# Fused two-block transformer on one core: steps beside the first input product laid out by time

## The reference

```
z = rms_norm(x, norm_mix) @ w_in
y_a = rg_lru_mixer(...)        # conv of 4, two sigmoid gates, a linear scan, times gelu(gate)
y_b = short_conv_mixer(...)    # conv of 3
y_c = fox_mixer(...)           # 4 heads, causal attention with a forget gate
y_d = nsa_mixer(...)           # 4 heads: compressed, selected and window attention, gated and summed
x = x + concat(rms_norm(each)) @ w_out
x = x + ffn(x)
```

```
blocks = kx[:, idx] + pos
hid = gelu(einsum('bnld,ldm->bnm', blocks, w1));  kc = rms_norm(hid @ w2)
p_c = masked_softmax(q @ kc * scale + rel_bias, dist_c >= 0);  o_c = p_c @ vc
```

## Time and profile before

| | |
|---|---|
| median of 3 runs | 3336.67 us (3329.39 to 3336.78) |
| profiled execution | 3337.88 us |
| its span | 3335.9 us |
| PE, PE weight load, DVE, ACT, POOL busy | 96%, 74%, 59%, 34%, 47% |
| mean granted clock of PE | 0.985 |
| DMA | 286.03 MB, mean 86 GB/s |

### The profile page before, as it was taken

How to read it: one execution, slowest core, us unless ns; L and a number is a source line. 1 busy time by engine, 2 the same in 40 slices (tenths; PEclk the granted TensorE clock), 3 DMA queues, 4 the chain that set the end, 5 groups by cost and what they waited for, 6 DMA issues and landing times. The chain is left out here.

```text
span 3335.9 us, 35062 instructions
## 1 busy us (share of the span) xinstructions
PE 3210.7 (96%) x13881; PEld 2471.9 (74%) x13881; DVE 1979.4 (59%) x2907; ACT 1135.4 (34%) x1686; POOL 1575.2 (47%) x764
## 2 busy tenths in 40 slices
PE   8889999998999999999999998898999999899999
PEld 5657888865778877777878776676778876587887
DVE  5464111288776584449477723423686588877756
ACT  5453222345422235543222322322322235542222
POOL 3224544566454453335554523433454556645454
PEclk9999999999999999999999999999999999999999
DMA  4212333321232333223332312222232332123232
GB/s 176 67 45 76 101 95 97 93 70 51 78 102 87 97 99 108 86 67 91 99 101 86 116 51 64 70 63 70 70 101 89 95 95 71 49 82 101 89 95 89
DMA packets 80675, 286.03 MB, mean 86 GB/s; under 512 B 9088, under 2 KB 9344, under 8 KB 80384
## 3 DMA queue, kind: packets, MB, share of 16 engines
q1 hardware_dynamic: 80512, 283.80, 27.2%
HBM read 281.40 MB, written 2.10 MB: 85 GB/s over the span
## 5 line engine op out<-in xcount | busy, mean ns | idle before, releaser
L2149 POOL TENSOR_TENSOR WL<-RAW,WH 128x1024 fp32r<-128x1024 f32 x504 | 1243.4, 2470 | 1362.1 <-ACT WH L1461 1361.6
L1243 PE MATMUL PS<-XH,WH 128*128 128x512 f32 x2768 | 1135.7, 410 | 44.2 <-POOL WL L2149 38.8
L1245 PE MATMUL PS<-XH,WL 128*128 128x512 f32 x2768 | 1088.0, 393 | 0.0
L1244 PE MATMUL PS<-XL,WH 128*128 128x512 f32 x2768 | 1087.8, 393 | 0.0
L1243 PEld LDWEIGHTS PS<-XH,WH 128*128 128x128 f32 x2768 | 525.5, 190 | 221.1 <-issue 89.7
L1461 ACT ACTIVATE WH<-RAW 128x1024 fp32r<-128x1024 f32 x504 | 526.5, 1049 | 430.6 <-PE PS L1245 430.0
L1244 PEld LDWEIGHTS PS<-XL,WH 128*128 128x128 f32 x2768 | 526.1, 190 | 114.6 <-issue 14.2
L1245 PEld LDWEIGHTS PS<-XH,WL 128*128 128x128 f32 x2768 | 525.0, 190 | 114.0
L1243 PE MATMUL PS<-HH,WH 128*128 128x512 f32 x1264 | 500.9, 396 | 15.4 <-DVE HL L2046 9.6
L1244 PE MATMUL PS<-HL,WH 128*128 128x512 f32 x1264 | 494.4, 391 | 0.0
L1245 PE MATMUL PS<-HH,WL 128*128 128x512 f32 x1264 | 494.3, 391 | 0.0
(11 more groups left out here) (225 smaller groups left out, 2359.3 us busy)
## 6 DMA issues: line engine op xcount, KB each, us to landing
RAW<-wst SPq DMA_DIRECT2D x504, 512.0 KB, 3.5
BI<-natb SPq DMA_DIRECT2D x16, 384.0 KB, 4.6
X<-xin SPq DMA_DIRECT2D x16, 256.0 KB, 5.0
X<-cmpw SPq DMA_DIRECT2D x1, 2048.0 KB, 9.5
out<-X SPq DMA_DIRECT2D x8, 256.0 KB, 2.1
BI<-relm SPq DMA_DIRECT2D x4, 448.0 KB, 10.0
PRM<-prm SPq DMA_DIRECT2D x1, 685.0 KB, 12.4
BI<-rope SPq DMA_DIRECT2D x2, 256.0 KB, 4.0
```

Of the source, the lines that this page charges most:

```text
L1243: e.matmul(o, wh, h, start=first, stop=False)
L1244: e.matmul(o, wh, l, start=False, stop=False)
L1245: t = e.matmul(o, wl, h, start=False, stop=last)
L2149: e.tensor_tensor(WL[:, b % NSPLIT, :], RAW[:, b % NRAW, :], WH[:, b % NSPLIT, :].bitcast(f32), SUB).then_inc(*did(lo_made, ("lo", b)))
```

## The change

- `later(..., first=True)` no longer appends: it inserts a step into `soon` by its due tile.
- `head_norm`: the second half is due after 5 tiles, was 3. `lru_gates` after 8, was 3. The swap of the nsa keys after 7, was 4.
- `attend`: `scores(n)` is now the last of the four steps of a beat.
- `cmp_blocks` becomes four steps `cmp_block`, each a memset and two sums, due after 2, 6, 10 and 14 tiles; the four products are due after 22 to 25 tiles, were 12, and the step after them (`cmp_kv`) after 28, was 3 (it stood behind the products in the queue).
- `cmp_turn` loses its DVE part to a new step `cmp_soft`, which runs beside beat 4; `cmp_turn` stays beside beat 6.

```diff
             def later(fn, delay=3, first=False):
-                (soon if first else bg).append((state["tile"] + delay, fn))
+                due = state["tile"] + delay
+                if not first:
+                    bg.append((due, fn))
+                    return
+                n = len(soon)
+                while n and soon[n - 1][0] > due:
+                    n -= 1
+                soon.insert(n, (due, fn))
...
-                later(go, first=True)
+                later(go, 5, first=True)
...
                 def beat(n):
                     def f():
-                        if n < len(units):
-                            scores(n)
                         if 0 <= n - 3 < len(units):
                             values(n - 3)
                         if 0 <= n - 2 < len(units):
                             turn(n - 2)
                         if 0 <= n - 1 < len(units):
                             normalise(n - 1)
+                        if n < len(units):
+                            scores(n)
...
-                    later(lru_gates, first=True)
+                    later(lru_gates, 8, first=True)
...
                     blk = [tiles.get() for _ in range(4)]
-                    i0 = step("cmp_blocks", b.ap, z, [s.ap for s in blk], [x for s in blk for x in s.free])
-                    b.done((i0, "blk"))
+                    laid = {}
+
+                    def block(l0):
+                        def f():
+                            s = blk[l0 // 8]
+                            i = step("cmp_block", l0, b.ap, z, s.ap, s.free)
+                            laid[l0] = (i, "blk")
+                            if l0 == 24:
+                                b.done((i, "blk"))
+                        return f
...
                     for l0 in range(0, 32, 8):
-                        later(product(l0), 12)
-                    later(go)
+                        later(block(l0), 2 + l0 // 2, first=True)
+                    for l0 in range(0, 32, 8):
+                        later(product(l0), 22 + l0 // 8)
+                    later(go, 28)
...
-                    later(swap, 4, first=True)
+                    later(swap, 7, first=True)
...
+                def cmp_soft():
+                    sc, sm, rc, made = cmp["a"]
+                    i = step("cmp_soft", c, sc.ap, sm, rc, made, st["gt"])
+                    cmp["a"] = (sc, (i, "p"))
+
                 def cmp_turn():
-                    sc, sm, rc, made = cmp["a"]
+                    sc, made = cmp["a"]
...
-                attend(units, (4, 3)[c], {1: cmp_scores, 6: cmp_turn, 10: cmp_values})
+                attend(units, (4, 3)[c], {1: cmp_scores, 4: cmp_soft, 6: cmp_turn, 10: cmp_values})
...
-            def cmp_blocks(i, b, made, blk, free):
+            def cmp_block(i, l0, b, made, blk, free):
                 pos = PRM[:, POFF["cmp_pos"]:POFF["cmp_pos"] + 32]
                 for event in free:
                     w.wait_ge(*at(event))
-                for s in blk:
-                    ins = e.memset(s, 0.0)
-                ins.then_inc(*did(dve_made, (i, "zero")))
+                e.memset(blk, 0.0).then_inc(*did(dve_made, (i, "zero")))
...
-            def cmp_turn(i, c, sc, sm, rc, made, gt, bks, pcs):
+            def cmp_soft(i, c, sc, sm, rc, made, gt):
                 pr = by31(sc[:, 0:256], 8)
```

More of the change, by code:

```diff
@@ L686, in f @@
                             bk = st["cb"]
-                            i = step("cmp_product", l0, bk.ap, bk.free, blk[l0 // 8].ap, (i0, "blk"))
+                            i = step("cmp_product", l0, bk.ap, bk.free, blk[l0 // 8].ap, laid[l0])
                             if l0 < 24:
@@ L760, in cmp_turn @@
                         pcs.append(pads.get())
-                    i = step("cmp_turn", c, sc.ap, sm, rc, made, st["gt"], [(bk.ap, bk.free) for bk in bks],
-                             [(pc.ap, pc.free) for pc in pcs])
+                    i = step("cmp_turn", sc.ap, made, [(bk.ap, bk.free) for bk in bks], [(pc.ap, pc.free) for pc in pcs])
                     for p in range(2):
@@ L1347, in cmp_product @@
                     w.wait_ge(*at("w1"))
-                    w.wait_ge(*at(made))
+                w.wait_ge(*at(made))
                 for l in range(l0, l0 + 8):
@@ L1381, in cmp_scores, with cmp_turn @@
                     t.then_inc(*did(pe_made, (i, "m", p)))
[L1383 removed]
+            def cmp_turn(i, sc, made, bks, pcs):
                 pr = by31(sc[:, 0:256], 8)
@@ L1387, in cmp_turn @@
                         w.wait_ge(*at(event))
-                    w.wait_ge(*at((i, "p")))
+                    w.wait_ge(*at(made))
                     for u in range(4):
@@ L1917, in cmp_blocks @@
                     w.wait_ge(*at(event))
-                for s in blk:
-                    ins = e.memset(s, 0.0)
-                ins.then_inc(*did(dve_made, (i, "zero")))
+                e.memset(blk, 0.0).then_inc(*did(dve_made, (i, "zero")))
                 w.wait_ge(*at(made))
                 w.wait_ge(*at((i, "zero")))
[L1923 to L1931, removed]
+                for br in range(2):
+                    r = slice(64 * br, 64 * br + 64)
+                    o = blk[r].rearrange("p (l n) -> p l n", n=64)[:, :, 32 * br:32 * br + 31]
+                    src = b[r, 16 * (l0 // 16):16 * (l0 // 16) + 496]
+                    src = src.rearrange("p (n l) -> p l n", l=16)[:, l0 % 16:l0 % 16 + 8, :]
+                    pp = pos[r, l0:l0 + 8].unsqueeze(2).to_broadcast([64, 8, 31])
+                    ins = e.tensor_tensor(o, src, pp, ADD)
                 ins.then_inc(*did(dve_made, (i, "blk")))
```

5 lines of the change are left out of this document (2 added, 3 removed).

## The result

| | before | changed |
|---|---|---|
| median | 3334.88 us (4 runs, 3329.39 to 3336.78) | 3314.52 us (4 runs, 3313.54 to 3315.47) |
| profiled execution | 3337.88 us | 3315.47 us |
| its span | 3335.9 us | 3313.6 us |
| mean granted clock of PE | 0.985 | 0.988 |

The ratio is 0.9942, with a 95% interval of 0.9924 to 0.9959: the changed kernel is faster, by 20.4 us in the medians and 22.3 us between the two spans. The forecast was 3308.5 us in a range of 3301 to 3320, with 28.2 us saved: the median came 6.0 us above it. It was counted from the median of the first three runs of the kernel before (3336.67 us); the fourth run (3333.08 us) lowered that median, so the two medians differ by less than the spans do.

The account below looks back on a forecast made before the run. TensorE (PE), busy 96% of the span, was taken as the bound, with gains only from its waits and clock. Seven terms sum to 28.2 us off the profiled 3337.9, giving 3309.7, or a median of 3308.5 us; range 3301 to 3320.

Parts of the forecast that it names:

- (a): First input product: head norms two tiles later remove most of two waits for the square and both clock drops, 6.9 us saved.
- (b): Compressed blocks on DVE in four pieces instead of one: PE's 6.1 us stop and what follows it go, 9.3 us saved.
- (e): First nsa beat moved from tile 92 to 96: of a 1.4 us wait for a head gain, 0.8 us saved.
- (f): Lru gates at tile 120 instead of 115: cost falls from 9.9 to 8.9 us, 1.0 us saved.
- T: The time when PE reaches tile 120, from which the forecast counted ACT's and PE's steps behind the lru gates.
- (c): Compressed softmax two beats ahead: the second head pair's 5.8 us stop near tile 152 and its clock loss go, 7.8 us saved.
- (d): Scores last in a beat: values and turns no longer wait behind that beat's reduction and exp, 1.2 us saved.
- (g): NAT layer, tiles 1499 to 1676: norms two tiles later cover the first norm's wait for the square, 1.2 us saved.
- the first (more left standing): Rival: 1 us waits at five more beats and a later ACT at the lru gates give back 9 to 10 us, 3318.5; chance 0.16.

Follow-up runs that it names:

- u_norm: Changed kernel with the head norm's second half due after 3 tiles again instead of 5: 3315.66 us.
- u_blocks: Changed kernel with all four compressed blocks laid in one piece at tile 64 again: 3321.46 us.
- u_lru: Changed kernel with the lru gates due after 3 tiles again instead of 8 (tile 115): 3312.32 us.
- v_lru9: Changed kernel with the lru gates due one tile later (9 instead of 8), behind the beat of tile 120: 3314.28 us.
- w1: Changed kernel with the lru gates and roots cut into two steps, one per half of the channels, at tiles 113 and 121, scans at 118 and 128: 3310.54 us.
- w5: w1 with ROOM 4 instead of 7, the first scan moved behind the beat of tile 124 and the second a tile later: 3311.23 us, ratio 0.9931.
- u_soft: Changed kernel with the compressed softmax again in beat 6, right ahead of its turn: 3326.35 us.
- u_scores: Changed kernel with the scores first in a beat again: 3321.43 us.
- w2: w1 with head norms at 6 tiles instead of 5 and the fox output norm two tiles later: 3308.76 us.
- v_best: v_chain with head norms a tile later (6) and output norms two tiles later: 3311.09 us.
- v_chain: Changed kernel with ROOM 4 instead of 7, lru gates due after 9 tiles instead of 8, and both scans six tiles later: 3311.7 us.

## Why the forecast came out high in its gain

The direction and the range held; 5.4 us of the 28.2 did not come (22.8 measured from tile 9 on). By the forecast's own parts:

**(a) head norms.** Tiles 9 to 36 saved 2.93 us of 3.0: the wait went from 2.01 to 0.62, and the clock drop went. At tile 101 no wait at all, as said. u_norm gave back 4.0 us, but only 1.8 of them at tile 27, and there without a clock drop behind a longer stop (2.41 us). So that the 2.01 us stop of the kernel before was followed by a drop is in its rows, but not that such a stop must be. The sizes forecast were right; that u_norm met its 4 us was luck.

**(b), (e) blocks and the first nsa beat,** with the second norm of (a) (tiles 36 to 105). 12.6 of 14.0. The stop of 6.08 us at tile 69 is gone and nothing took its place there; the 1.44 of (e) went whole, not 0.8 (+0.6). Against that stands a wait that was not foreseen, 1.26 us at tile 83, and drops worth 4.0 instead of 4.8 us. Before, the four compressed products lay on PE at tiles 79 to 84 and gave the fox output norm's sum time; the forecast moved them and asked only whether their blocks would be ready, not what they had been covering. DVE of the changed kernel there:

```profile
105.54 0.48 DVE L1939 MEMSET TT<- 128x512 f32 x1
106.06 1.18 DVE L1948 TENSOR_TENSOR TT<-TT,PRM 64x248 f32<-64x248 f32 x2
107.27 0.69 DVE L1933 COPY TT<-PS 128x512 f32<-128x512 f32 x1
108.66 0.69 DVE L1824 TENSOR_TENSOR TT<-TT 128x512 f32<-128x512 f32 x1 [0.69 <-ACT TT L1521]
```

The fourth block stands in that queue too, but does not make most of the wait: with all blocks at tile 64 it was still 0.79 us (u_blocks). That the missing cover makes the rest was not tried by itself.

**(f) lru gates.** The largest miss: 1.0 saved was forecast, 1.9 lost. The mechanism was right, and undoing it (u_lru) and moving it (v_lru9, w1) bear it out. ACT and PE of the changed kernel, T being 165.05 us:

```profile
167.90 1.28 ACT L1585 ACT_TABLE_LOAD   x1
...
172.86 1.28 ACT L1475 ACT_TABLE_LOAD   x1
174.15 0.72 ACT L1598 ACTIVATE TT<-TT,SM 128x512 f32<-128x512 f32 x1
...
177.99 1.04 ACT L1482 ACTIVATE WH<-RAW 128x1024 fp32r<-128x1024 f32 x1
178.94 0.57 ACT L1541 ACTIVATE PT<-PS 128x512 f32<-128x512 f32 x1
```

```profile
179.56 1.12 PE L1321 MATMUL PS<-PT,TT 128*64 128x128 f32 x8 [6.20 <-ACT PT L1541]
...
182.60 0.69 PE L1313 MATMUL PS<-CST,PT 128*128 128x128 f32 x2 [1.92 <-DVE PT L1798]
...
184.37 0.63 PE L1264 MATMUL PS<-XH,WH 128*128 128x512 f32 x1
```

ACT was free at T + 2.9 (forecast 1.9), its copy landed at T + 14.5 (13.9), PE came at T + 8.3 (7.8): a stop of 6.20 us against 6.1. The two loads of 1.28 us again have an activation 0.02 us behind them, as before. The Trainium skill, ScalarE: Activation LUTs, section What ACT_TABLE_LOAD costs, has about 1380 ns of drain beside each load; these rows don't agree with it either.

Two sizes were off. First, the turn behind it waited 1.92 us and not 1.0, and this is why:

```profile
180.57 0.15 DVE L1790 RECIPROCAL SM<-SM 128x2 f32<-128x2 f32 x1
180.76 1.79 DVE L1798 TENSOR_SCALAR PT<-PT,SM,GT 128x128 f32<-128x128 f32 x2
```

```profile
179.11 3.10 POOL L2166 TENSOR_TENSOR WL<-RAW,WH 128x1024 fp32r<-128x1024 f32 x1 [15.11 <-ACT WH L1482]
```

The normalisation took 1.79 us where the same rows take 0.60 in u_lru and w1; it ended 0.34 us behind POOL's subtraction, which ran until 182.21. The weight split that ACT does just ahead of the copy starts that subtraction just then. The repeat shows the same 1.79. The Trainium skill, SBUF — State Buffer, section Who interferes with whom, says that VectorE, in a mode that uses both of its ports, and GpSimd lock one shared pair of SBUF ports against each other, and that the second to start is blocked until the first is done; the rows agree with it, though none shows in which mode the normalisation ran. The forecast's list held the right row at its undisturbed length.
Second, the clock. In w5, where no drop falls between tiles 105 and 129, that stretch has 31.9 us besides its waits. The kernel before has 34.4 there, the changed one 34.2: drops of 2.5 and 2.3 us. I had 3.6 for the two of before and 1.8 for the one of after. With waits of 6.3 before and 8.4 after, the stretch costs 8.8 and 10.7 us over full speed, where the forecast had 9.9 and 8.9: the difference is the 1.9 us lost. The repeat of the changed kernel shows 42.2 us for the stretch, so 1.5 lost; against the 1.0 saved that was forecast the miss is 2.5 to 2.9 us.

**(c) compressed softmax.** 7.5 of 7.8: 5.84 went, 0.43 came at tile 157 (0.6 forecast). The size was right for this pair; u_soft shows a value of 12.4 us, because the first pair would have waited 5.9 us too once the blocks, the taps and the gates had moved.

**(d) scores last.** 1.34 of 1.2 where its gain was read, by the net result. But u_scores makes it 7.1 us. Besides the waits of before that came back (0.47, 1.19) it shows 2.27 us at tile 69, 0.6 more each at tiles 112 and 124 (8.71 against 6.20 + 1.92) and 1.3 at 157, all of them at places whose gain the forecast had booked to (b), (c) and (f). The forecast gave the parts a value in one order of adding them; the sum was fair, the shares were not.

**(g) NAT.** This term failed, and landmarks show it. The rows are the first matmul of the layer's first weight tile and of the tile behind its last one, in the kernel before and in the changed kernel:

```profile
1250.04 0.39 PE L1243 MATMUL PS<-XH,WH 128*128 128x512 f32 x1
...
1461.26 0.40 PE L1243 MATMUL PS<-HH,WH 128*128 128x512 f32 x1
```

```profile
1227.78 0.39 PE L1264 MATMUL PS<-XH,WH 128*128 128x512 f32 x1
...
1439.24 0.39 PE L1264 MATMUL PS<-HH,WH 128*128 128x512 f32 x1
```

That is 211.2 us before and 211.5 after (211.4 in the repeat), at a granted clock of 1.00. The wait of 1.2 us at the first norm went, and 24 tiles into the layer 1.3 us were gained; but from there on each 24 tiles took 27.4 us instead of 27.2, which gave it back by the end of the 192. The three traces with the norms' tile moved again agree: 211.3 with the norms at three tiles (u_norm, where the 1.2 us wait is back), but 209.7 and 209.8 with them at six (w2, v_best). All eleven other traces lie between 211.2 and 211.5. So two tiles more saved nothing there, where 1.2 us was forecast; three tiles more saved 1.5 against the kernel before. Behind tile 185 as a whole the traces differ by up to 4.7 us (3055.1 in v_best to 3059.8 in the kernel before); 1.5 of these are the head norms in NAT.

Of the rivals, none was right as a whole; the first (more left standing) named the kind of loss. Its 1 us at five more beats did not come: 0.24 at tile 112, 0.43 at 157, and the 1.26 at 83.

## What to carry to other kernels

When work is moved off a place, ask what it was covering for others there, and not only whether its own inputs come in time. A chain of 10 us on a side engine, kept in one piece, stopped the main one at each place tried (6.2 us; 7.5; 2.76 with 3.71 behind it; 0.65 and 1.54 behind 3.9 for the taps). Cutting it in two lowered the stop (3.85, then 0.79), and the next thing to look at is what is queued behind the last piece (3.35). Compare such edits at a landmark behind them rather than by the total, since the far stretch alone differed by some 2.5 us in one order of work. Where an edit also reaches a later stage, set landmarks around that stage: the total hid that the NAT term brought nothing and that one tile more brought 1.7 us against the changed kernel. And a part's value when undone is not its value when added.

## What was not expected of the hardware

**The length of a stop does not tell whether the clock falls.** I took it that stops of 1.4 us leave it and stops of 2.0 us do not. Rows behind a stop, PE in order of time of u_norm, then a stretch of w5:

```profile
41.24 1.13 PE L1275 MATMUL PS<-TT,CST 128*128 128x512 f32 x2 [2.41 <-ACT TT L1511]
41.80 0.80 PE L1264 MATMUL PS<-XH,WH 128*128 128x512 f32 x1
42.43 0.39 PE L1265 MATMUL PS<-XL,WH 128*128 128x512 f32 x1
```

```profile
187.00:196.00 9.00, 7.18 (x37) 4.40 (x37) 5.23 (x13) 6.67 (x12) 2.52 (x2) 1.00 0.00 0
```

A stop of 2.41 us in u_norm, at the place where 2.01 us cost the kernel before its clock, left it at 2.4 GHz, and so did the 3.35 us of w5; 2.76 us in v_chain and 3.85 us in w1 were followed by matmuls 0.43 us apart, as this one of v_chain:

```profile
181.51 0.63 PE L1265 MATMUL PS<-XL,WH 128*128 128x512 f32 x1
```

The other bound fails too. In u_norm a stop of 1.48 us was followed by the lower clock, 1.6 us behind its end:

```profile
127.87 0.38 PE L1384 MATMUL PS<-TT,W 128*128 128x31 f32 x2 [1.48 <-DVE TT L1955]
...
129.83 0.63 PE L1266 MATMUL PS<-XH,WL 128*128 128x512 f32 x1
```

So 1.5 us of a forecast for such a stop are in doubt even when the stop is sized exactly. What decides it was not found.

**VectorE behind a GpSimd subtraction.** Besides the 1.79 us above: two block sums took 2.61 instead of 1.17 us in u_blocks, beginning 0.7 us into a subtraction (88.42 to 90.81). In a kernel with a subtraction every eight tiles, a short row that is waited for should be priced at both lengths.
